# A hybrid decoder step: twelve input projections moved between the memory's and the samples' attentions, the others dealt evenly

## What is computed

```python
z = rmsnorm(x, norm_mix) @ w_in            # 54 projections of 128 channels, over 1032 columns
o_lru = lru_branch(lru_x, lru_gate)        # recurrence over the prompt; 16 projections feed it
o_nsa = nsa_attend(q, ...)                 # 8 heads; three branches: selected, window, compressed
o_mem = softmax(mem_q @ mem_k.T * MEM_HD ** -0.5) @ mem_v     # 4 heads, 256 memory rows
z = (merge[:, :, 0] * (o_lru @ w_up_a) + merge[:, :, 1] * (o_nsa @ w_up_b)
     + merge[:, :, 2] * (o_mem @ w_up_m))  # merge = sigmoid of 24 of the projections
h = x + z @ w_o
y = h + (silu(f @ w_ffn_gate) * (f @ w_ffn_up)) @ w_ffn_down  # f = rmsnorm(h)
```

## Time and profile before

| what | value |
| --- | --- |
| time, median of 3 runs (lowest, highest) | 2675.66 us (2675.41, 2675.78) |
| the profiled execution: its time, its span | 2671.46 us, 2669.8 us |
| TensorE's granted clock over the span | 0.93 of 2.4 GHz |
| busy: PE, DVE, ACT, POOL | 2416.7 (91%), 1072.0 (40%), 724.7 (27%), 655.0 us (25%) |
| joined program, first to last step | 428.5 to 1333.6 us |
| middle program, last matmul before it to first behind it | 1333.6 to 1614.0 us |
| tail | 1614.0 to 2669.8 us |

### The profile page before, as it was taken

One profiled execution on the slowest core, in us unless ns is written; L12 is line 12 of the kernel. 1 busy time (PEld: TensorE's weight loads), 2 busy tenths in 40 slices (PEclk: granted clock), 3 DMA queues, 4 the chain that ended last, 5 costly groups with the idle time before them and its releaser, 6 DMA issues. The chain is left out here.

```text
span 2669.8 us, 37831 instructions
## 1 busy us (share of the span) xinstructions
PE 2416.7 (91%) x14415; PEld 2234.0 (84%) x14415; DVE 1072.0 (40%) x1945; ACT 724.7 (27%) x1319; POOL 655.0 (25%) x399
## 2 busy tenths in 40 slices
PE   7996877989989899899856587999999999999999
PEld 7995647789888788799733577999999999999999
DVE  5465014436255564655433003263333333333333
ACT  5222011242352544644332004232211111111111
POOL 2212001111111011010035001234444434433443
PEclk9997789999999899999678568999999999999999
DMA  5224424224233221110056626332111111111112
GB/s 178 88 80 168 125 72 147 67 67 128 64 97 88 74 63 52 60 49 28 6 125 181 160 65 246 104 119 91 61 48 47 40 47 47 47 39 47 47 47 79
DMA packets 136151, 226.26 MB, mean 85 GB/s; under 512 B 29418, under 2 KB 95098, under 8 KB 135420
## 3 DMA queue, kind: packets, MB, share of 16 engines
q1 hardware_dynamic: 122492, 194.57, 23.5%
q0 software_dynamic: 6560, 25.22, 3.2%
q10 hardware_dynamic: 6976, 4.79, 0.7%
HBM read 176.80 MB, written 55.08 MB: 87 GB/s over the span
## 5 line engine op out<-in xcount | busy, mean ns | idle before, releaser
L1101 PE MATMUL att_facc<-h_hi,att_w_hi 128*128 128x344 f32 x960 | 337.7, 352 | 57.8 <-DVE att_zf L1281 44.5
L2153 PE MATMUL tl_acc<-tl_x_hi,tl_w_hi 128*128 128x344 f32 x1632 | 348.0, 322 | 21.1 <-DVE tl_x_lo L2216 14.0
L2153 PE MATMUL tl_acc<-tl_x_lo,tl_w_hi 128*128 128x344 f32 x1632 | 347.2, 321 | 0.0
L2153 PE MATMUL tl_acc<-tl_x_hi,tl_w_lo 128*128 128x344 f32 x1632 | 345.4, 320 | 0.0
L1101 PE MATMUL att_facc<-h_lo,att_w_hi 128*128 128x344 f32 x960 | 314.5, 328 | 0.0
L1101 PE MATMUL att_facc<-h_hi,att_w_lo 128*128 128x344 f32 x960 | 314.2, 327 | 0.0
L2153 PEld LDWEIGHTS tl_acc<-tl_x_hi,tl_w_hi 128*128 128x128 f32 x1632 | 275.2, 189 | 22.5 <-issue 15.9
L2153 PEld LDWEIGHTS tl_acc<-tl_x_lo,tl_w_hi 128*128 128x128 f32 x1632 | 277.0, 189 | 0.0
L2153 PEld LDWEIGHTS tl_acc<-tl_x_hi,tl_w_lo 128*128 128x128 f32 x1632 | 272.6, 188 | 0.0
L2118 POOL TENSOR_TENSOR tl_w_lo<-tl_raw,tl_w_hi 128x1024 fp32r<-128x1024 f32 x64 | 153.9, 2404 | 425.1 <-ACT tl_w_hi L2059 425.1
L1101 PEld LDWEIGHTS att_facc<-h_hi,att_w_hi 128*128 128x128 f32 x960 | 187.7, 196 | 72.4 <-DVE att_zf L1281 42.2
(11 more groups left out here) (355 smaller groups left out, 4031.5 us busy)
## 6 DMA issues: line engine op xcount, KB each, us to landing
tl_raw<-in_w_ff SPq DMA_DIRECT2D x66, 512.0 KB, 3.6
z<-att_zf SPq DMA_DIRECT2D x120, 172.0 KB, 3.7
att_raw<-in_w_in SPq DMA_DIRECT2D x40, 512.0 KB, 4.3
tl_tmp<-z SPq DMA_DIRECT2D x24, 516.0 KB, 4.4
tl_raw<-in_w_up SPq DMA_DIRECT2D x16, 512.0 KB, 4.0
fr_raw<-in_w_in SPq DMA_DIRECT2D x14, 512.0 KB, 4.8
zn<-fr_x SPq DMA_DIRECT2D x10, 516.0 KB, 2.9
fr_x<-in_xT SPq DMA_DIRECT2D x8, 644.0 KB, 10.3
```

The source lines that it names most:

```text
L1101: mm = pe.matmul(facc[:, 0:CW], w[:, u % 2, k, :], h[:, k, c * CW:(c + 1) * CW], start=(x == 0), stop=(x == 23))
L2153: mm = pe.matmul(a[:, c, 0:CW], wt[:, s, k, :], x[:, x0, c * CW:(c + 1) * CW], start=first and n == 0, stop=last and n == 2)
```

## The change

Of the 40 projections of the joined program 28 stay; their ticks are dealt 2, 2, 1, 2, 1, 2, 1, 2 over all 192 steps (13 in 8 steps, 19.5 in a block of 12), behind the same 24 ahead. The other 12 (144 ticks) run in the middle program, whose three parts are written as one function, `memory_and_samples`: 4 ticks at its begin, 2 behind each of the 32 `turn(j)`, 3 behind each sample's key scores, 2 behind the group product, 1 behind each sample's memory scores, 2 behind the transposes, 3 behind each sample's values and 2 behind each sample's memory values. Their weights are issued and their outputs stored by POOL. The weight slots outlive the joined program, and it also loads and splits the first two units of the middle. W becomes 3, 33, 62, 92 and SIG 22, 52, 81, 128.

All keys and values of the samples come through one ring of ten slots, issued by SP alone: pages for the selected branch, single DMAs for the window and the memory. Two of the ring's items are issued in each pass of the loop over m, between that tile's constants and the store and load of the memory attention's `oT` and `q`, until the ten slots are full; the others behind the loop. The 24 output copies move to POOL in the joined program, one in each of the steps 24 to 47. Further: the new token's and the compressed keys are one operand, so that a sample's key scores take one matmul fewer; `normal(j)` stands before `maximum(j + 1)` on DVE and `turned(j)` and `output(j - 1)` before `exponentials(j + 1)` on ACT; and the order of the samples' small operations on DVE is another.

```diff
+FILL = 12
...
-    UNITS += list(range(U_MG, NU_IN))
-    NU = len(UNITS)
+    NU = len(UNITS) + NU_IN - FILL - U_MG
+    UNITS += list(range(U_MG, NU_IN - FILL + 2))
+    raw, w_hi, w_lo, zf = fill
     PRE = 24
-    TICKS = ((4,),) * 3 + ((2, 2, 2, 1, 1) * 4 + (2,) * 4,) * (QT - 3)
+    TICKS = ((2, 2, 1, 2, 1, 2, 1, 2),) * QT
...
+        c_out = per["soft"][7]
+        COPY = 24
+        copies = [(d["kvT"][n], src, False) for n, src in enumerate((d["z"][U_CMPK], d["z"][U_CMPV], d["zn"][0], d["z"][U_SELV],
+                                                                     d["zn"][1], d["z"][U_WINV]))]
+        for h in range(MH):
+            copies += [(d["memT"][h], d["memn"][h], False), (d["memT"][MH + h], d["memz"][MH + h], False)]
+        copies += [(d["win_out"][b, 0:WIN - 1], d["win_in"][b, 1:WIN], False) for b in range(NS)]
+        copies += [(d["win_out"][:, WIN - 1, j * P:(j + 1) * P].rearrange("b p -> p b"), src[:, NP_:T], True)
+                   for j, src in enumerate((d["zn"][1], d["z"][U_WINV]))]
...
+                if 0 <= J - COPY < len(copies):
+                    dst, src, slow = copies[J - COPY]
+                    pool.dma_start(dst, src, allow_slow_non_contiguous=slow).then_inc(c_out, 16)
...
+def memory_and_samples(nc, d, per, h_hi, h_lo, fill):
...
+    points = [("begin", 0)] + [("mat", j) for j in range(NJ)] + [("ks", b) for b in range(NS)] + [("grp", 0)]
+    points += [("km", b) for b in range(NS)] + [("turn", 0)] + [("vs", b) for b in range(NS)] + [("vm", b) for b in range(NS)]
+    DEAL = {"begin": 4, "mat": 2, "ks": 3, "grp": 2, "km": 1, "turn": 2, "vs": 3, "vm": 2}
+    ticks, done = {}, 0
+    for p in points:
+        ticks[p] = list(range(done, done + DEAL[p[0]]))
+        done += DEAL[p[0]]
+    assert done == 12 * FILL
...
+    ITEMS = []
+    for b in range(0, NS, 2):
+        ITEMS += [("ks", b), ("ks", b + 1), ("kw", b)]
+    ITEMS += [("km", b) for b in range(NS)]
+    for b in range(0, NS, 2):
+        ITEMS += [("vs", b), ("vs", b + 1), ("vw", b)]
+    ITEMS += [("vm", b) for b in range(NS)]
+    with ExitStack() as ctx:
...
+            def q_load(m):
+                if m >= 2:
+                    sp.wait_ge(s_mm, MH * (m - 1))
+                sp.dma_start(q[:, m % 2], tile_of(d["zn"][6:10], m)).then_inc(q_in[m % 2], 16)
+            def o_store(m):
+                sp.wait_ge(s_oe, MH * (m + 1))
+                sp.dma_start(tile_of(d["o_mem"], m), oT[:, m % 2]).then_inc(o_out[m % 2], 16)
+            def ring_load(i):
+                kind, b = ITEMS[i]
+                slot, landed = ring[:, i % NR], r_in[i % NR]
+                if i >= NR:
+                    was, of = ITEMS[i - NR]
+                    read = {"k": mk_mm if was == "km" else k_mm, "v": mo_mm if was == "vm" else o_mm}[was[0]]
+                    sp.wait_ge(read, of + (2 if was[1] == "w" else 1))
+                if kind in ("ks", "vs"):
+                    with sp.Fori(0, PAGES) as x:
+                        page = sp.value_load(pt[0:1, bass.ds(x + b * PAGES, 1)], min_val=0, max_val=src.shape[0] - 1)
+                        sp.dma_start(slot.rearrange("p (a n) -> p a n", n=P)[:, bass.ds(x, 1), :].rearrange("p a n -> p (a n)"),
+                                     src[bass.ds(page, 1)].rearrange("a p n -> p (a n)")).then_inc(landed, 16)
...
+            loaded = 0
+            for m in range(QT):
+                constants(m)
+                for i in range(loaded, min(NR, loaded + 2)):
+                    ring_load(i)
+                    loaded += 1
+                if m >= 2:
+                    o_store(m - 2)
+                if m + 2 < QT:
+                    q_load(m + 2)
+            o_store(QT - 2)
+            o_store(QT - 1)
+            for i in range(loaded, len(ITEMS)):
+                ring_load(i)
+            sp.wait_ge(o_done, 2)
...
+            def filler(p):
+                for tick in ticks[p]:
+                    u, c, g, x0 = tick // 12, tick // 4 % 3, tick // 4, 6 * (tick % 4)
+                    if tick % 12 == 0 and u >= 2:
+                        pe.wait_ge(f_lo, u - 1)
+                    if x0 == 0 and g:
+                        pe.wait_ge(f_ev, g)
...
                 turn(j)
+                filler(("mat", j))
...
+            for b in range(NS):
+                sample_scores(b)
+                filler(("ks", b))
...
+            pe.wait_ge(vn_in, 16 * 2 * NS)
+            for b in range(NS):
+                sample_values(b)
+                filler(("vs", b))
...
+            for b in range(NS):
+                memory_values(b)
+                filler(("vm", b))
...
+            def output(j):
+                m, h = j // MH, j % MH
+                if h == 0 and m >= 2:
+                    act.wait_ge(o_out[m % 2], 16 * (m // 2))
+                act.wait_ge(s_pv, j + 1)
+                act.activation(oT[:, m % 2, h], O[j % 2][:, 0:P], ACT.Copy).then_inc(s_oe, 1)
...
+            def evict(p):
+                for g in chunks[p]:
+                    if g >= 4:
+                        dve.wait_ge(f_out[g % 4], 16 * (g // 4))
+                    c = g % 3
+                    dve.wait_ge(f_mm, g + 1)
+                    dve.tensor_tensor(zf[:, g % 4], facc[:, 0:CW], per["rstd"][:, c * CW:(c + 1) * CW], ALU.mult).then_inc(f_ev, 1)
...
-        values_of(sp, (0, 1, 2, 3, 4, 6))
...
-    @block.gpsimd
-    def _(pool):
-        pool.wait_ge(pt_in, 16)
-        for b in range(NS):
-            pool.dma_start(kw[:, b], d["winkT"][b]).then_inc(k_in[b], 16)
-            pages(pool, b, d["sel_kT"], ks[:, b], k_in[b])
...
-        values_of(act, (5, 7))
...
-            start_phase(nc, part, block, "att2")
-            sample_attention(nc, d, per, part, block, bank)
-            outputs(nc, d, block, per["soft"][30])
-            sample_memory(nc, d, per, part, block, bank)
+            with ExitStack() as rest:
+                sbw = sb_of(nc, rest, "w")
+                fill = (sbw("raw", [P, 2, KT, P]), sbw("hi", [P, 2, KT, P], F32R), sbw("lo", [P, 2, KT, P], F32R),
+                        sbw("zf", [P, 4, CW]))
+                attention_and_recurrence(nc, d, per, h_hi, h_lo, fill)
```

780 lines of the change are left out of this document (395 added, 385 removed).

## The result

The changed kernel takes 2739.13 us, the median of 3 runs (2723.63 to 2740.32), against 2675.66: 2.22% more, with an interval of 1.78% to 2.66%: slower. The profiled execution is the one of 2723.63, 52.2 us over that of before; the forecast was 2683.7 and 2640 to 2719. Run again on another chip it took 2736.39 (2716.04 to 2741.30, 5 runs), ratio 1.0224 (1.0201 to 1.0246).

What follows compares the result with a forecast made beforehand. The prediction took PE to set the joined program's pace and SP's page issuing to hold up much of the middle. Joined program -114 and middle +122 gave +8 us, so 2683.7 us, range 2640 to 2719.

Steps and rivals of the forecast that it cites:

- The next eight blocks: Joined program, eight blocks after the first six: ticks go from 160 to 156, so -4 us.
- The first six blocks: Start of the joined program: 171 of 288 ticks go, 298 us against 415.8, so -118 us.
- the 80 us: First six blocks: recurrence pieces no longer hidden under ticks, and transposes' waits, add 80 us to PE's 212 us.
- The last two blocks: End of the joined program: 39 ticks where there were 8, 100 us against 92, so +8 us.
- the -114: Whole joined program: its three stretches together change by -114 us, bounds -150 to -89.
- The middle: Middle program, memory attention through memory values: 402.8 us against 280.4, so +122 us, bounds +105 to +149.
- SP's chain of issues: Middle program: SP issues all pages, 12.1 us per sample's eight; memory attention ends at 170 us, value samples landed at 319.
- the stalls at `q` of tile 2 and at the turns: Memory's attention: waits behind SP's page issues make it end at 170 us instead of some 125, so 45 us show.
- the clock in the memory's values: Memory's values in the middle: 34 to 58 us for eight samples, taken as 42, nearer to the high clock.
- B: Middle program: SP's issuing stays hidden, some 310 us, +30; with -114 the time is 2592; chance 0.10.
- C: Joined program: DVE and ACT set most steps and the clock falls; gain -89, net +33, 2709 us; chance 0.20.
- D: Joined program: slack absorbs the recurrence's long steps, 45 of 80 us show; gains 149, net -27, 2649 us; chance 0.20.

Runs made afterwards that it cites:

- the aligned table: Changed kernel with ticks dealt 2, 2, 2, 1, 1 four times and then four 2s, so chunks of four end with a step: 2689.79 us.
- the aligned table with the recurrence in place: Changed kernel with ticks dealt so chunks end with a step, W and SIG kept at the changed kernel's steps: 2685.26 us.
- the small ticks: Changed kernel with only the first of the six matmuls of each tick in the middle program: 2677.12 us.

## Why the prediction was wrong, point by point

**The step that failed** is "The next eight blocks go from 160 to 156 ticks: -4". It priced the number of ticks and not where a chunk of four ends. It should have counted, from the table, the steps in which one chunk ends and the next begins: none before, 30 after, 15 of them in these blocks. The view of waits showed the tick's wait for the eviction already before, 7 times and 19.0 us in these blocks, and the eviction's place in DVE's order was in the code. Measured: +26.8 us in these blocks for the -4, and 45 us in the joined program, shown by the aligned table (-45), by the aligned table with the recurrence in place (778.0 for 777.5 us) and, the other way, by 17 such places in the kernel before (+31.6 in the trace's eight blocks). That the places cost it is shown; how a place's cost divides into DVE's lateness, the eviction itself and the clock is shown only in part.

**The first six blocks**, -118, measured -116.0, were right by luck. The sum had 212 us of PE's work, 6 for the clock and 80 of time in which PE waits. Measured are 241.8 us busy at a clock of 0.87 and 58.0 idle: the busy time was 24 too small and the idle time 22 too large. Eleven of the places lie here. Aligned these blocks take 283.1 us with three ticks more, where the same sum gives 301, so the 80 us were some 18 too many, and the places made good for it. The last two blocks, +8 forecast and +8.1 measured, came as summed, PE busy 94.4 us at a clock of 1.00; the aligned run's +2 there says nothing of places, for its table leaves them 32 ticks for 39. Without the 30 places the joined program would have given back 127.6 us (905.1 to 777.5), 14 more than the -114.

**The middle**, +122, measured +127.2 in the trace. SP's chain of issues holds within 4 us at each point shown, the stalls at `q` of tile 2 and at the turns sum to 44.5 us for 45, and the small ticks show that the pages alone set the value samples. Mis-sized was the clock in the memory's values: 42 us were taken, between 34 and 58; the profiled execution has 37.4. If the longer and more frequent executions have the 58 of the aligned run's trace, 16 over the forecast, that explains why the median lies 15.5 us over the profiled time; it is inferred, as said above. The evictions of the middle's ticks wait 13.0 us in all, which I had at 0.2 a j.

**The sum for the median**: 8 forecast, 31 for the eight blocks, 16 for the memory's values at the low clock, 10 for the rest of the middle (127.2 + 4.6 for the memory's values' 37.4 instead of 42, less 122), 2 for the first six: +67, against the +63.5 measured. Two of the prediction's own sums are off by less than 1 us, which changes nothing: 13.7 and twice 12.1 are 37.9 and not 38.6, and 2671.46 and 8 are 2679.5 and not 2679.9.

**The rivals.** B (issuing hidden) is refuted: the first two samples' value pages took SP 25.9 us to issue, and with nearly no ticks PE still waited for them. By the Trainium skill ("DMA: Bandwidth & Descriptors", section "Issuing engines are not separate DMA queues") several issuers save only sequencer time that is usually small; here a second issuer took 12 us from the values and GpSimd's share 14 us from the attention, so for 64 KB pages it was not small. C had the joined program's gain nearly right (-89, measured -81). Of its two causes the clock is borne out, 0.87 in the first six blocks and 0.91 even aligned; that DVE and ACT set the step is not borne out as the main cause, for with the same work on both the aligned table alone takes 45 us away. D's mechanism, that long steps are absorbed, is partly true: by the count above some 62 of the 80 us show when aligned, under the 67 that D named; the 30 places hid it.

The measured time lies 20 us above the range. None of the prediction's rivals was about the pattern of the table.

## What to carry to other kernels

When filler work with a single accumulator is dealt over steps, count the places where one unit of it ends and the next begins inside a step: all that is queued behind the filler then waits for the eviction, at best for its own 0.7 us and at worst for an evicting engine that is late by a whole step, and the clock fell with these waits. Here it was some 1.5 to 2 us a place in all. Deal it in a pattern whose sums meet the unit's size at step ends. And when transfers that are issued in loops are put on one queue, follow that queue issue by issue and ask for each short store or load behind a loop who waits for it; two bounds of nearly one length hide each other. Here the values kept their 89 us when most of the ticks' work was gone, and lost 12 when a second engine issued pages.
